# Layer 1's attention over the latent keys made inside layer 0's gather, the rest merged afterwards

## The reference

```python
# layer 0: a mixer (Fourier groups and state-space heads), then the mixer "peer" over all 768 tokens
x_lat, x_ctx = x_lat + g2 * ff[:512], x_ctx + cg2 * ff[512:]
# layer 1: latent attention; 16 heads, query and key of 96 (64 + 32 rotary), value of 64
q = apply_rope(rms_norm((rms_norm(dq, q_a_norm) @ w_uq).reshape(..., 16, 96), q_norm))
kv = (rms_norm(dkv[..., :256], kv_a_norm) @ w_ukv).reshape(..., 16, 128)
k = rms_norm(concatenate([kv[..., :64], k_pe]), k_norm)     # latent keys are rotated, context keys not
k_all, v_all = concatenate([k_context, k_latent]), concatenate([v_context, v_latent])
s = einsum("bqhd,bkhd->bhqk", q, k_all) * 96 ** -0.5
out = softmax(s) @ v_all                                    # only for the 512 latent queries
x_lat = x_lat + g1 * (out @ w_o)
# then "peer" over the 512 latent tokens: each token takes, for each of 8 heads, 16 experts out of 16384
y = sum over experts of gate * gelu(h . u_expert) * v_expert
```

## Time and profile before

| what | value |
|---|---|
| median of 3 runs | 4237.56 us (4237.34 to 4241.53) |
| the profiled execution | 4237.69 us, its span 4235.9 us |
| PE, DVE, ACT, POOL busy | 72%, 68%, 31%, 36% of the span |
| mean granted TensorE clock | 0.861 of full speed |
| layer 0's gather | first issue 573.9 us, last products from 2611.1 us |
| attention's first product | 2684.0 us |
| layer 1's first gather issue | 2900.5 us |

### The profile page before, as it was taken

The page is one execution under the profiler, slowest core; times in us unless marked ns, Lnnn a source line. Parts: engine busy times, 40 slices in busy tenths (PEclk is TensorE's granted clock), DMA queues, the critical chain, the costliest instruction groups (busy, mean ns, idle before and its releaser), DMA issues. The chain is left out here.

```text
span 4235.9 us, 38223 instructions
## 1 busy us (share of the span) xinstructions
PE 3033.1 (72%) x11918; PEld 1230.6 (29%) x11918; DVE 2865.7 (68%) x7196; ACT 1292.3 (31%) x3543; POOL 1514.5 (36%) x1352
## 2 busy tenths in 40 slices
PE   8999899766676755555666677999876644655555
PEld 4655444322222211111112222565322211111111
DVE  2426857988888897555555665666888998555555
ACT  2125423433333332112222453663333322111111
POOL 0002213544444444444443441002444544444442
PEclk9999999988888977777778888999987888777777
DMA  4114759999999999999999997107999999999998
GB/s 179 42 39 180 295 222 365 414 420 420 420 420 398 420 421 419 421 421 417 420 421 417 421 421 273 40 1 271 419 420 420 421 421 420 416 422 421 417 421 351
DMA packets 234015, 1481.27 MB, mean 350 GB/s; under 512 B 26060, under 2 KB 37548, under 8 KB 63572
## 3 DMA queue, kind: packets, MB, share of 16 engines
q0 software_dynamic: 184320, 1342.26, 76.5%
q1 hardware_dynamic: 48116, 132.61, 8.5%
q10 hardware_dynamic: 1376, 3.96, 0.2%
HBM read 1473.31 MB, written 5.42 MB: 349 GB/s over the span
## 5 line engine op out<-in xcount | busy, mean ns | idle before, releaser
L2206 PE MATMUL banks<-arena 128*64 128x512 f32 x5104 | 1611.5, 774 | 1139.2 <-ACT arena L2472 1060.4
L1914 POOL DMA_INDIRECT arena<-experts,arena x1280 | 1454.7, 1137 | 2245.7 <-PE banks L2206 1598.3
L2651 DVE CUSTOM_DVE_ANT_0 arena<-arena 128x1024 f32<-128x1024 f32 x1280 | 1541.4, 1224 | 877.4 <-DMA arena<-experts,arena 875.6
L2206 PEld LDWEIGHTS banks<-arena 128*64 128x64 f32 x5104 | 394.0, 167 | 2256.6 <-ACT arena L2472 1547.9
L2466 ACT ACTIVATE arena<-arena 128x2 f32<-128x2 f32 x638 | 129.5, 203 | 2189.9 <-DVE arena L2651 2189.6
L2472 ACT ACTIVATE arena<-arena 128x64 f32<-128x64 f32 x1276 | 374.7, 340 | 77.1 <-ACT arena L2466 2.8
L2007 PE MATMUL banks<-arena 128*128 128x512 f32 (+3 forms) x960 | 287.4, 454 | 0.8 <-DVE arena L2557 0.7
L453 PE MATMUL banks<-arena 128*128 128x512 f32 (+1 forms) x640 | 208.6, 486 | 1.9 <-ACT arena L514 1.9
L1934 PE MATMUL banks<-arena 128*128 128x512 f32 x416 | 189.9, 605 | 6.6 <-DMA arena<-l_w_out 3.0
L2007 PEld LDWEIGHTS banks<-arena 128*128 128x128 f32 x960 | 160.2, 191 | 108.2 <-issue 87.8
L453 PEld LDWEIGHTS banks<-arena 128*128 128x128 f32 x640 | 120.7, 190 | 86.1 <-issue 77.6
(11 more groups left out here) (273 smaller groups left out, 3054.0 us busy)
## 6 DMA issues: line engine op xcount, KB each, us to landing
arena<-l_w_ada SPq DMA_DIRECT2D x48, 1024.0 KB, 8.4
arena<-wq SPq DMA_DIRECT2D x54, 512.0 KB, 7.9
arena<-experts,arena POOLq DMA_INDIRECT x1280, 22.2
arena<-l_w_in SPq DMA_DIRECT2D x6, 2048.0 KB, 8.0
arena<-l_w_out SPq DMA_DIRECT2D x4, 1536.0 KB, 14.3
arena<-l_w_o SPq DMA_DIRECT2D x4, 1024.0 KB, 8.3
arena<-keys SPq DMA_DIRECT2D x27, 128.0 KB, 10.4
arena<-gates SPq DMA_DIRECT2D x6, 512.0 KB, 12.3
```

The source lines that it names most:

```text
L1914: pool.indirect_dma_start(slots[n], None, tbl, bass.IndirectOffsetOnAxis(ap=expert[:, ring[c], k:k + 1], axis=0)).then_inc(land[n]["sem"], ...
L2206: mm = pe.matmul(core["ps"][QS * j:QS * j + QS, c, :], diag[:, g % 2, k, :], v[:, D + c * 512:D + (c + 1) * 512], start=(g % (NB * PH) == ...
L2651: dve.tensor_tensor_reduce(u, u, rep[i // PH % 2][:, k % NQ, :], 1.0, 0.0, ALU.mult, ALU.add, dots[:, k:k + 1]).then_inc(dot["sem"], up(dot))
```

## The change

The softmax over 768 keys is split in two parts that are merged: the 512 latent keys, whose tiles 0 to 3 are ready long before the gather of layer 0 ends, and the 256 context keys (tiles 4 and 5).

1. Inside layer 0's gather, counted in half steps h (h = 2g and 2g + 1): 32 items at h = 284 + 3i (eight pairs of heads; for each two query items and two key items, each of two tiles), and 32 steps at h = 300 + 3j (a pair of heads and a query tile over 512 keys): scores, peak, exponentials, turn, product with the values, turn back, rows. Not normalised outputs ("partials"), peaks and sums are kept; queries and partials are stored in DRAM, pair by pair. The stages of an item and a step follow half by half.
2. From fetch 384 (g = 96) on, slots 6 to 9 are given up and eight remain; their memory holds the early work's data. `PREP_AT` becomes 97, 106, 115, 129, 161.
3. After the gather only the keys of tiles 4 and 5 are made, in eight chunks of four heads at h = 389 to 401, beside tile 5's preparation and the last early steps (four scores, h = 384 to 393). Queries and partials are loaded back once tile 5's down product is done.
4. `attention` runs 16 units m (two heads, two query tiles, 256 keys: 1024 score columns). The peak is joined with the early one; DVE scales, POOL makes a diagonal from the weight of the early part, PE adds early output times diagonal.

```diff
+DOWN_LAST = RO + SLOT
+ITEM_AT = [284 + 3 * i for i in range(4 * PAIRS)]
+STEP_AT = [300 + 3 * j for j in range(TL * PAIRS)]
+KEY_AT = [389, 391, 393, 395, 398, 399, 400, 401]
+LAST_HALF = KEY_AT[-1] + 5
-PREP_AT = (130, 139, 148, 157, 168)
+PREP_AT = (97, 106, 115, 129, 161)
+     "near": 2, "halved": range(2, PH), "narrow": (BATCH * 96, (6, 7, 8, 9)),
...
+    def early_score(pe, j):
+        u, q = divmod(j, TL)
+        pe.wait_ge(co["sem"], at(co, 4 * u + 4))
+        if j:
+            pe.wait_ge(ec["sem"], at(ec, j))
+        for a in range(2):
+            i = pe.matmul(core["ps"][:, 4 + a, :], eq[u % 2][0:QK, a, q * P:(q + 1) * P], ek[u % 2][0:QK, a, :],
+                          start=True, stop=True)
+        i.then_inc(es["sem"], up(es))
...
+    def tensor(pe, h):
+        product, turn = find(KEY_AT, h, 0, 4)
+        if turn is not None:
+            key_turn(pe, turn)
+        if product is not None:
+            key_product(pe, product)
+        score, probabilities, weigh, output = find(STEP_AT, h, 0, 2, 4, 5)
+        product, turn = find(ITEM_AT, h, 0, 4)
+        if output is not None:
+            early_output_turn(pe, output)
+        if probabilities is not None:
+            early_turn(pe, probabilities)
+        if weigh is not None:
+            early_weigh(pe, weigh)
+        if score is not None:
+            early_score(pe, score)
+        if turn is not None:
+            item_turn(pe, turn)
+        if product is not None:
+            item_product(pe, product)
+
+    def scalar(act, h):
+        squares, root, columns = find(KEY_AT, h, 1, 2, 5)
...
+        exponentials, probabilities = find(STEP_AT, h, 1, 3)
+        copy, root, columns = find(ITEM_AT, h, 1, 2, 6)
+        if columns is not None:
+            item_columns(act, columns)
+        if copy is not None:
+            item_copy(act, copy)
+        if probabilities is not None:
+            early_copy(act, probabilities)
+        if exponentials is not None:
+            early_exponentials(act, exponentials)
+        if root is not None:
+            item_root(act, root)
+
+    def vector(dve, h):
...
+        peak, out, stored = find(STEP_AT, h, 1, 5, 6)
+        level, ready = find(ITEM_AT, h, 2, 3)
+        if peak is not None:
+            early_peak(dve, peak)
+        if level is not None:
+            item_level(dve, level)
+        if ready is not None:
+            item_rows(dve, ready)
+        if out is not None:
+            early_out(dve, out)
+        if stored is not None:
+            early_rows(dve, stored)
...
@@ attention, PE
+        for m in range(UNITS):
+            score(m)
+            if m >= 1:
+                turn(m - 1)
+            if m >= 2:
+                weigh(m - 2)
@@ attention, DVE
+        for m in range(UNITS + 3):
+            if m < UNITS:
+                peak(m)
+            if 1 <= m <= UNITS:
+                normalise(m - 1)
+            if m >= 3:
+                out(m - 3)
@@ attention, POOL
+        for m in range(UNITS):
+            pool.wait_ge(iv["sem"], at(iv, 4 * m + 4))
...
+            pool.tensor_tensor(diag[m % 2], ident(core).unsqueeze(1).to_broadcast([P, 4, P]),
+                               bcast(four(be, m), P), ALU.mult).then_inc(dr["sem"], up(dr))
@@ peer_block, the same on PE, ACT and DVE
+                if n == 2 * NQ - 1 and early(2 * g):
+                    up_tensor(pe, 2 * g)
...
                 for u, p in preps(g):
                     prepare(u, p)
+                if early(2 * g + 1):
+                    up_tensor(pe, 2 * g + 1)
             if layer == 0:
-                up_tensor(pe, lambda p: prepare(TT - 1, p))
+                for h in range(2 * POS, LAST_HALF + 1):
+                    prepare(TT - 1, h - 2 * POS)
+                    up_tensor(pe, h)
```

More of the change, by code:

```diff
@@ L1098, in latent_up @@
+KEY_AT = [389, 391, 393, 395, 398, 399, 400, 401]
+KEY_BANKS = [2, 0, 1, 2, 4, 5, 0, 1]
+LAST_HALF = KEY_AT[-1] + 5
 def latent_up(core):
     nc = core["nc"]
[L1103 to L1109, removed]
@@ L1110, in latent_up @@
-    wkv = view(core, UP_KV, 2, MH * (NOPE + MV))
-    rowb = view(core, RO + 8704, 3, NH * QK)
+    NH = 4
+    NI = len(ITEM_AT)
+    QW = 2 * QK
+    scale = QK ** -0.5
+    wq = view(core, E_WQ, 3, QW)
+    wkv = view(core, E_WKV, 2, PAIR_W).rearrange("p k (h c) -> p k h c", c=P)
+    rows = [view(core, o, 4 * QK) for o in E_ROW]
+    rot = [view(core, o, 4, 16) for o in E_ROT]
+    eq = [view(core, o, 2, LAT) for o in E_QUERIES]
+    ek = [view(core, o, 2, LAT) for o in E_KEYS]
+    ev = [view(core, o, TL, 2 * MV) for o in E_VALUES]
@@ L1147, in latent_up, with item @@
[L1147 to L1163, removed]
-        else:
[L1165 to L1168, removed]
+    def item(i):
+        u, r = divmod(i, 4)
+        return u, r // 2, r % 2
@@ L1195, in query_columns, with item_columns @@
-    def query_columns(act, i):
+        act.activation(rs[:, i % 3, 0:4], ss[:, i % 3, 0:4], ACT.Sqrt).then_inc(ro["sem"], up(ro))
+    def item_columns(act, i):
+        u, kind, tp = item(i)
         act.wait_ge(tr["sem"], at(tr, i + 1))
-        if i:
-            act.wait_ge(spilled["sem"], at(spilled, 16 * i))
-        else:
[L1200 to L1213, removed]
+        act.wait_ge(ld["sem"], at(ld, 48))
+        if u >= 2:
+            act.wait_ge(es["sem"], at(es, TL * (u - 1)))
+            if kind == 0:
+                act.wait_ge(qsp["sem"], at(qsp, 16 * (u - 1)))
@@ new lines, in item_columns, with item_level @@
+        o = (eq, ek)[kind][u % 2].rearrange("p h (t l) -> p t h l", l=P)
+        act.activation(o[0:QK, 2 * tp:2 * tp + 2],
+                       core["ps"][0:QK, 2, :].rearrange("p (t h l) -> p t h l", t=2, h=2), ACT.Copy,
+                       scale=column[0:QK, kind:kind + 1]).then_inc(co["sem"], up(co))
+    def item_level(dve, i):
+        u, kind, tp = item(i)
+        S = ss[:, i % 3, 0:4]
+        dve.wait_ge(sd["sem"], at(sd, 2 * i + 2))
+        if kind == 0:
+            dve.tensor_scalar(S, S, share, eps, ALU.mult, ALU.add).then_inc(sr["sem"], up(sr))
+        else:
+            for j in range(2):
+                t = 2 * tp + j
+                lv = dve.tensor_scalar(S[:, 2 * j:2 * j + 2], S[:, 2 * j:2 * j + 2], share, pe2[:, t:t + 1],
+                                       ALU.mult, ALU.add)
+            lv.then_inc(sr["sem"], up(sr))
@@ L1214, in query_rows, with item_rows @@
+    def item_rows(dve, i):
+        u, kind, tp = item(i)
+        R = rs[:, i % 3, 0:4]
+        row = rows[i % 2].rearrange("p (g c) -> p g c", c=QK)
         dve.wait_ge(ro["sem"], at(ro, i + 1))
@@ L1225, in query_rows @@
[L1225 to L1268, removed]
@@ L1382, in attention @@
[L1382 to L1385 removed]
+    one = view(core, ONE_O, PAIRS, TL, P)
+    pr = [view(core, L0 + 7168 + n * 1024, 4, CTX) for n in range(2)]
+    pt = [view(core, L0 + 15616 + n * 1024, TC, 2, 2 * P) for n in range(2)]
+    diag = [view(core, L0 + 17664 + n * 512, 4, P) for n in range(2)]
+    nm1 = view(core, S_EARLY + 64, 4 * UNITS)
@@ L1386, in attention @@
+    sm1 = view(core, S_EARLY + 128, 4 * UNITS)
+    top, nm, al, sm, su, rc, be, part = (view(core, MISC + 512 + i * 4 * UNITS, 4 * UNITS) for i in range(8))
     sc = signal(core, "scores_ready")
@@ L1437, in weigh @@
             i.then_inc(pv["sem"], up(pv))
-        for n in range(N):
-            score(n)
-            if n >= 2:
-                turn(n - 2)
-            if n >= 7 and n % 4 == 3:
-                weigh(n // 4 - 1)
-        pe.wait_ge(ex["sem"], at(ex, N - 1))
-        project(0, 0, 0, 3)
-        turn(N - 2)
-        project(0, 0, 3, 5)
-        turn(N - 1)
-        project(0, 0, 5, 7)
+        for m in range(UNITS):
+            score(m)
+            if m >= 1:
+                turn(m - 1)
+            if m >= 2:
+                weigh(m - 2)
@@ L1451, in tensor @@
+        pe.wait_ge(ex["sem"], at(ex, 4 * (UNITS - 1)))
+        pe.wait_ge(oo["sem"], at(oo, UNITS - 4))
+        project(0, 0, 0, 6)
+        turn(UNITS - 1)
+        weigh(UNITS - 2)
+        pe.wait_ge(oo["sem"], at(oo, UNITS - 2))
+        project(0, 0, 6, 7)
         weigh(UNITS - 1)
@@ L1502 @@
+    return load, tensor, vector, scalar, gpsimd
 ROWS = 2 * D
@@ L1790, in peer_block, with early, place @@
     SCALED = {0: 6, 1: 7, 2: 9, 4: 11, 5: 12, 3: 13}
-    def items(g):
-        return [Q_AT.index(g - s) if layer == 0 and g - s in Q_AT else None for s in range(5)]
+    def early(h):
+        return layer == 0 and h >= ITEM_AT[0]
+    def place(u):
+        return (xps[0], hps[0], 4) if u < TL else (xps[1], hps[1], 6)
     def preps(g):
@@ new lines, in _ @@
+                load_queries(0)
+                load_pair_keys(0)
+                sp.wait_ge(rd["sem"], at(rd, TL))
+                sp.dma_start(g2, gate_rows(core, layer, 1, 1)).then_inc(g2l["sem"], up(g2l, 16))
+                for u in range(PAIRS):
+                    if u + 1 < PAIRS:
+                        load_queries(u + 1)
```

(7 more changed lines are left out.)

700 lines of the change are left out of this document (447 added, 253 removed).

## The result

The changed kernel takes 4310.0 us (median of 4 runs, 4307.9 to 4314.7), the kernel before 4238.6 in the same runs: ratio 1.0169, 95% interval 1.0151 to 1.0187. It is 71 us slower. I had forecast slower, 4274 us, inside a range of 4195 to 4330: direction and range hold, the size of the move is half of the measured one (36 of 71 us).

What follows compares the result with a forecast made beforehand. DMA was taken as always busy in layer 0's gather, PE 99% busy in attention. From 4237.7 us, plus 83 (gather), minus 9 (end of layer 0), minus 38 (attention), gave 4274 us, range 4195 to 4330.

Steps and rivals of the forecast that it cites:

- the reload: End of layer 0: loading back queries and partials (5.2 MB, 12.5 us) starts at 30.5 us and is covered.
- the slow clock in attention: Attention: PE idle 3.5 us per turn makes products run at 1.2 GHz, 1.4 us per turn, 13 turns.
- the stretch before attention: End of layer 0, without gathers: about 60 us instead of 69.4, 9 us gained; not being shorter would show the prediction wrong.
- The gather loses 83 us by an order ring: Layer 0's gather: a 17.8 us ring against 14.94 us of supply, 74 us over 26 turns; 74 + 5 + 9 - 5.
- Tile 4's down product: Layer 0's gather: one half of it (4.6 us) stands in front of third 2's turn, costing 5 us.
- The eight buffers: Layer 0's gather: 3 us lost at each of three tile ends, 9 us; their depth absorbs 5 us once.
- The DMA share would be near 0.85: Sign in layer 0's gather, half 300 to 380: DMA share near 0.85 instead of 1.01.
- The ring of 7.9 us: Attention: score, DVE work, turn and weighing in a row take 7.9 us per unit, 131 us for sixteen before slowing.
- Rival 1: Gather and attention: clock stays at 2.4 GHz as added work fills PE; 4220 us, faster; chance 0.19.
- Rival 2: Layer 0's gather hides all early work, a ring under 15 us; 4210 us; chance 0.10.
- Rival 3: Attention: GpSimd and DVE exclude each other, 16 x 1.5 = 24 us more, 4298 us; chance 0.07.
- Rival 4: Gather: slower clock and late buffers feed each other, ring 19.5 us, loss 128 us, 4319 us; chance 0.10.

Runs made afterwards that it cites:

- the third experiment: Changed kernel with queries and all but the last pair's partials reloaded before that pair's store on SP: 4294.0 us, 16 us less than the changed kernel.
- both filler runs: Changed kernel with unused PE products filling idle stretches: in attention, before each turn, 4277.7 us; in the gather, behind 14 of 26 steps' weighing, 4282.9 us.

## Why the prediction was right in direction and wrong in size

By the spans 41 us were missing: 77 us longer where 36 were forecast. Of these 6.5 lie in the gather, 13.3 in the end of layer 0, 19.0 in attention, 2.2 elsewhere. The steps that failed are the reload, a term that the prediction put at nothing, and the slow clock in attention, a term that it made too small. One of its own signs of being wrong came true: the stretch before attention isn't shorter.

- *The gather loses 83 us by an order ring.* Right: 89.5. The ring was forecast at 17.8 us; without its two longest turns the 24 others took 18.0 us on average, with three half steps of dot products as the measure. Tile 4's down product was sized at 5 us for one of its halves; both fell into one turn, of 25.5 us, 7.5 above the average. The other long turn, of 24.3 us, holds tile 4's end, where PE waits for the addition, 6.3 us above the average where 3 were put down. PE at the tile's end and at the two halves:
```profile
2315.22 3.68 PE L2470 MATMUL banks<-arena 128*64 128x512 f32 x8 [7.26 <-DVE arena L2927]
...
2410.97 6.00 PE L2307 MATMUL banks<-arena 128*128 128x512 f32 x16
...
2426.82 4.79 PE L2307 MATMUL banks<-arena 128*128 128x512 f32 x16
```
The eight buffers were sized at 9 us less 5, and measured alone 3.6.
- *The DMA share would be near 0.85.* Wrong as a sign, right in the bytes: the share is 0.93, but 358 GB/s are 0.86 of 416. The busy share fell by 7% where the bytes fell by 14%.
- *"The reload of queries and partial outputs ... starts at 30.5 and is covered."* This step failed. I had the loads start at the down product that frees their memory, and left out what stands before them on SP: the store of the last pair, which waits for the last early step, 18 us later, at 2754.2. The rest of that stretch was nearly right (57.8 for 59 us), though the terms listed up to the start of the down product add up to 18.2 us and not 19, and it started after 20.1. The price of uncovered loads was too low as well: PE waited 15.9 us where up to 12.5 were put down. It cost the 13 us of this stretch, and the third experiment gives 16 us back by the order on SP alone.
- *"I take 1.4 us per turn"* for the clock in attention. This step failed in size. The ring of 7.9 us was right: 8.0 with the clock held up. The slow clock was mis-sized: 2.3 us a unit, as it lasted through turn (1.97 for 1.0) and weighing (2.8 for 1.45) and into the score (2.1 for 1.85). I had taken the size from gather halves with 1.94 us of products; here 4.3 us of work stood behind the idle stretch. Fourteen units of 2.3 us are 32, thirteen of 1.4 were 18: that is 14 us of the 19. Another 3.4 lie at the start of the stretch, where the first scores took 7.05 us at the low clock that 15.9 us of waiting had left (3.69 us with the reload earlier). The rest, 1.6 us, is open.
- Rival 1 (clock at 2.4 GHz throughout) is refuted by the clock of 0.87 and 0.71; its premise, that the clock decides some 2 us per turn of either ring, holds in both filler runs. Rival 2 (all hidden) is refuted by 358 GB/s. Rival 3's mechanism is there, but not its cost. The Trainium skill, SBUF — State Buffer, "Who interferes with whom", has one of the two wait for the other's whole instruction. The trace agrees: GpSimd's operation took 1.04 us alone (1.5 were estimated) and 1.96 us behind the scaling, and in all 60 places of four runs where it overlapped a scaling it ended 2.11 to 2.13 us after the scaling's start, whether it began 0.16, 0.23 or 0.65 us behind it. DVE came first, as the prediction had held against the rival: its scaling took 1.22 us, as its 1024 elements did elsewhere, the wait fell on GpSimd, and the ring came to its 8.0 us. That GpSimd before DVE would lengthen a turn was not tried. Rival 4's price (4319) came near the median by luck: it had 128 us lost in the gather and a ring of 19.5 us, where 89.5 and 18.0 were measured.

The change itself held up: with two orders on the engines and one on SP written otherwise, the same split of attention is about 87 us faster than the kernel before (ratio 0.9796), not 71 us slower.

## What to carry to other kernels

When work is moved under a stretch that another resource limits, add up not only each engine's time but the longest ring through the engines' queues, with the table loads that stand in it; put what waits for nothing (a root, a store, a load) where an engine would wait anyway, and let the consumer run one unit later than the producer. A wait on one queue is part of the price of everything behind it, DMAs on SP included. Idle stretches of PE of about 3.5 us cost twice in these runs: once as such, and once as slow products behind them.

## What the runs showed of the hardware

- Behind 3.5 us of idle PE products ran at 1.2 GHz (3.68 for 1.94 us; in attention through 4.7 us of work); in 2 of 15 such places in attention they began at 2.4 GHz and fell to 1.2 about 1 us later. Behind 0.4 to 0.7 us of idle PE they ran at 2.4 GHz. After 2.06 us both occur: 2.53 us in one run and place, 1.94, 3.13 and 2.64 in three turns of another.
- Filling the stretch with products whose result nobody reads pays: 2.3 us for each unit of attention, 1.9 us for each turn in the gather.
- With the DMA engines 0.93 busy, 14% fewer bytes were moved than with 1.00 (358 and 416 GB/s), and during the reload 256 GB/s with 1.03.
- GpSimd's operation on 512 elements waits for DVE's scaling of 1024 that began up to 0.65 us before it: it ends 2.11 to 2.13 us after the scaling's start, wherever it starts itself. Its record includes the wait (1.47 to 1.96 us for 1.04), so that the two records overlap in time.
